# Moving tiles of the 256-column stages begin 128 bytes, not 192, past the weights' position modulo 256

## The chip, the cores and the metric

The kernel runs on one core of a Trainium2 chip. The metric is the device time of one execution in microseconds (us); the number compared is the median of several executions. The core has TensorE (PE; it loads a 128 x 128 tile of weights into its array, which the trace shows on a row of its own as PEld, and streams a moving tile past it), VectorE (DVE), ScalarE (ACT), GpSimd (POOL) and SyncE (SP), which issues most of the DMAs. Tensors in the on-chip memory have 128 partitions; an address below is the byte position in every partition.

## The reference, cut to what matters

Two transformer-like blocks over 256 tokens of width 1024. The first has one layer; the second has two layers and a second stream of 256 context tokens, which goes along through the first of them and feeds keys and values in the second. The weight products, which are nearly all of the matrix work:

```python
x = x + 0.5 * (silu(n(x) @ w_gate) * (n(x) @ w_up)) @ w_down      # 1024 -> 2816 -> 1024, six times
proj = h @ w_in[l]; ...; x = x + concat([o_a, o_b]) @ w_out[l]    # a mixer in each layer
```

The products and the result are float32.

## The kernel before, in words

**Products in three parts.** Each float32 operand is held as a high part of dtype float32r and a low part, the remainder. A weight tile of 128 x 128 meets a moving tile of 128 x n in three matmuls: high weights by high moving tile (L1464), high weights by low moving tile (L1465), low weights by high moving tile (L1466). The kind `pair` does the same on L1479 to L1481 for the first two outputs of a stage. Each matmul of the program has its own weight load, and the load of the next matmul runs beside the current one.

**Weights.** They stream from HBM in units of up to 1024 columns (`UC`) into `w_raw`, and are split by ACT (L1785) into `w_hi` and by DVE (L2085) into `w_lo`, three slots each. Most units are eight tiles of 128 columns, so tiles begin at multiples of 512 bytes. Exceptions are tiles of 96 columns (queries and keys of the second block) and of 16 (the decay projection, L1498 to L1500).

**Moving tiles.** `U` holds the normed activations, high part (`HI`) and low part (`LO`), in one of two views: `U0` and `U1`. `HH...` and `HL...` hold the hidden layer of a feed-forward part. Stages with 256 columns (one stream: the whole first block, and the second layer of the second block from its mixer on) use view `U0` and a hidden tensor allocated behind a spacer, `shift`. Stages with 512 columns (both streams) use `U1` and no spacer. For a few steps at each seam between 512-column stages the two halves of 256 columns are done one after the other, from the same unshifted tiles.

**Where tiles begin.** Tensors are allocated one behind the other, and the others before these are all whole multiples of 256 bytes long, so `U`, `w_hi` and `w_lo` begin at the same position modulo 256 (128). Within `U`, `U0` begins 48 floats, 192 bytes, later; a spacer of 48 floats does the same to the hidden tensors `f1`, `f2` and `f21`, and to the mixer tensors of the last layer (`M1`: `AC`, `FO`, `CV`, `CK`, `Y` and others). Below, **offset** means: start of the moving tile less start of the weight tile, modulo 256. It is 192 in the 256-column stages, 0 in the 512-column stages and their seams. Where the operands change places (`v_mm`, L1532 to L1534: the weights' tile moves, `U0` is loaded), the offset is 64. In `decay_mm` the 16-column weight tiles lie 64 bytes apart, so the offset goes through 192, 128, 64 and 0.

**Order of the stages.** f1 (us 16 to 198 of the profiled span), mixer 1 (to 466, with much work that is no weight product), f2 (to 651), then with 512 columns f10, mixer of layer 0, f20, f11 (to 2197), then with 256 columns mixer of layer 1 (to 2484) and f21 (to 2676). A feed-forward part is 44 outputs of 8 tiles and 8 outputs of 22 tiles, times three: 1,584 matmuls. A seam's halves have the same lines in the trace as everything else.

**What sets the order of work.** Plan writes all steps out in one list, and each engine goes through that list in order; waits are on semaphores between engines. Nothing in the list depends on addresses.

Of the kernel before, what the change touches and what calls it, by code (L numbers as in the profile page):

```python
# [9 lines left out]
F32 = mybir.dt.float32  # L10
# [1243 lines left out]
def build(nc, wstream, cols, consts, consts2, bias, xin, cvec, out):  # L1254
    with ExitStack() as stack:
        program(Plan(), nc, stack, wstream, cols, consts, consts2, bias, xin, cvec, out)


def program(plan, nc, stack, wstream, cols, consts, consts2, bias, xin, cvec, out):
    S = Signals()  # L1260
    up, at, landed = S.up, S.at, S.landed

    def sb(name, shape, dt=F32, st=None):
        return (st or stack).enter_context(nc.sbuf_tensor(name, shape, dt))

    X = sb("X", [128, 8, 512])
    U = sb("U", [128, 2 * 4096 + 64], F32R)
# [16 lines left out]

    HI = {f"U{i}": U[:, 48 - 48 * i:4144 - 48 * i].rearrange("p (k t) -> p k t", k=8) for i in range(2)}
    LO = {f"U{i}": U[:, 4144 - 48 * i:8240 - 48 * i].rearrange("p (k t) -> p k t", k=8) for i in range(2)}

    HI["UO"], LO["UO"] = HI["U0"][:, :, 256:512], LO["U0"][:, :, 256:512]  # L1290

    def shift(n, name, st):
        if n == 256:
            sb("S" + name, [128, 48], F32, st)

    def hidden(p, n):
        with ExitStack() as st:
            shift(n, p, st)
            HI[p], LO[p] = sb("HH" + p, [128, NF, n], F32R, st), sb("HL" + p, [128, NF, n], F32R, st)

    def halves(name, shape, st):
        HI[name], LO[name] = sb(name + "H", shape, F32R, st), sb(name + "L", shape, F32R, st)

# [22 lines left out]
    for l in range(2):  # L1326
# [4 lines left out]
        t2 = {}  # L1331
        with ExitStack() as st:
            shift(n, f"M{l}", st)

            t2["OT"] = []
            for half, x in (HI, "H"), (LO, "L"):
                with ExitStack() as s2:
# [5 lines left out]
            with ExitStack() as s2:  # L1343
                t2["VC"] = sb(f"VC{l}", [128, wide], F32, s2)[:, 0:3 * ns * 286].rearrange("p (c s t) -> p c s t", c=3, s=ns)
                t2["AC"] = sb(f"AC{l}", [128, 3, ns, 256], F32, s2)
            HI[f"CV{l}"] = sb(f"CVH{l}", [128, wide], F32R, st)[:, 0:3 * n].rearrange("p (c t) -> p c t", c=3)
            LO[f"CV{l}"] = sb(f"CVL{l}", [128, 3, n], F32R, st)
            def merged():
                HI[f"Y{l}"] = sb(f"Y{l}H", [128, 8, n], F32R, st)
                with ExitStack() as s4:  # L1350
                    t2["Y"] = sb(f"Y{l}", [128, 8, n], F32, s4)
                LO[f"Y{l}"] = sb(f"Y{l}L", [128, 8, n], F32R, st)

# [1274 lines left out]
```

## Time and profile before

| | us |
|---|---|
| median of 3 runs | 2685.14 |
| lowest and highest | 2680.0 and 2686.18 |
| time of the profiled execution | 2686.26 |
| its span, first to last instruction | 2684.4 |
| PE busy in it | 2594.5 (97%) |
| mean granted clock of TensorE | 0.989 |

How to read the rows further below. In the timeline a row is one matmul: start in us, duration in us, engine, line, output and inputs, count. Durations overlap, since a matmul starts while the one before is still draining; the distance from start to start is what a matmul costs when they stand one behind the other. A window's row gives its length, then for each engine busy us and number of instructions, then PE's granted clock, the DMA share and GB/s; the counts include the two or three instructions that were under way when the window began. A group's row gives line, engine, output and inputs, weight tile's and moving tile's size, count, busy us, mean ns of one, and idle time before them with what ended it. The chain is the work that ended last, followed back, in shares of the stretch by engine and line.

### The profile page before, as it was taken

How to read it: one execution, taken by the hardware profiler on the slowest of the kernel's cores; microseconds unless marked ns; L12 is line 12 of the kernel's file. 1: busy time of each engine (PE TensorE's matmuls, PEld its weight loads, DVE VectorE, ACT ScalarE, POOL GpSimd, SP SyncE). 2: the span in 40 equal slices, each digit the busy share in tenths (PEclk: the TensorE clock that was granted, in tenths of full speed). 3: DMA queues.
4: the chain of work that ended last, by engine and by line, in shares of the span. 5: the costliest groups of instructions: out<-in, count | busy, mean ns of one | idle time of the engine just before them, and what ended most of it. 6: DMA issues, size and time to landing. Idle time of an engine off the chain costs nothing.

```text
span 2684.4 us, 38719 instructions
## 1 busy us (share of the span) xinstructions
PE 2594.5 (97%) x15836; PEld 2299.7 (86%) x15836; DVE 1679.0 (63%) x2665; ACT 1094.6 (41%) x1707; POOL 64.1 (2%) x60
## 2 busy tenths in 40 slices
PE   7999898999999999999999999999999999998998
PEld 7998797999888888778888888889888888888998
DVE  6767545777677555666545767665555456776654
ACT  5446654555322224343244332224232234655543
POOL 0001030000000000000100000000000000000000
PEclk9999999999999999999999999999999999999999
DMA  7764202675555442112222455543443433244454
GB/s 262 236 231 174 88 9 72 212 237 174 167 187 190 158 143 94 51 40 87 93 89 94 149 180 185 176 159 111 146 133 130 141 110 103 74 142 161 161 181 146
DMA packets 110113, 380.98 MB, mean 142 GB/s; under 512 B 12016, under 2 KB 17392, under 8 KB 109552
## 3 DMA queue, kind: packets, MB, share of 16 engines
q1 hardware_dynamic: 108928, 373.32, 41.9%
q10 hardware_dynamic: 1008, 5.18, 0.5%
q8 instruction: 126, 2.06, 0.3%
q14 instruction: 51, 0.42, 0.1%
HBM read 377.40 MB, written 1.05 MB: 141 GB/s over the span
## 4 chain that ended last, share of the span: by engine, by line
PE 89%; DVE 5%; ACT 3%; issue 2%; DMA 0%; SPq 0%; ACTq 0%; DVEq 0%
PE B L1464 26%; PE B L1466 25%; PE B L1465 25%; ACT w_hi L1785 2%; DVE w_lo L2085 2%; PE B L1724 1%; PE B L1707 1%; PE B L1479 1%; PE B L1618 1%; PE B L1480 1%; PE B L1481 1%; PE B L1631 1%; PE B L1714 1%; DVE AC L2330 1%; DVE TMP L2112 0%
## 5 line engine op out<-in xcount | busy, mean ns | idle before, releaser
L1464 PE MATMUL B<-U,w_hi 128*128 128x256 f32 (+1 forms) x2896 | 961.7, 332 | 8.1 <-DVE w_lo L2085 8.0
L1465 PE MATMUL B<-U,w_hi 128*128 128x256 f32 (+1 forms) x2896 | 952.3, 329 | 0.0
L1466 PE MATMUL B<-U,w_lo 128*128 128x256 f32 (+1 forms) x2896 | 952.1, 329 | 0.0
L2085 DVE TENSOR_TENSOR w_lo<-w_raw,w_hi 128x1024 fp32r<-128x1024 f32 (+3 forms) x587 | 685.4, 1180 | 408.8 <-ACT w_hi L1785 407.7
L1785 ACT ACTIVATE w_hi<-w_raw 128x1024 fp32r<-128x1024 f32 (+3 forms) x587 | 590.8, 1012 | 505.3 <-PE B L1466 482.6
L1464 PEld LDWEIGHTS B<-U,w_hi 128*128 128x128 f32 x2896 | 546.1, 189 | 64.6 <-issue 8.1
L1465 PEld LDWEIGHTS B<-U,w_hi 128*128 128x128 f32 x2896 | 547.0, 189 | 53.7 <-issue 2.2
L1466 PEld LDWEIGHTS B<-U,w_lo 128*128 128x128 f32 x2896 | 545.6, 188 | 51.7
L1464 PE MATMUL B<-HHf,w_hi 128*128 128x256 f32 (+1 forms) x1122 | 364.6, 325 | 1.6 <-DVE w_lo L2085 1.6
L1466 PE MATMUL B<-HHf,w_lo 128*128 128x256 f32 (+1 forms) x1122 | 363.8, 324 | 0.0
L1465 PE MATMUL B<-HLf,w_hi 128*128 128x256 f32 (+1 forms) x1122 | 363.8, 324 | 0.0
L1848 ACT ACTIVATE HHf<-TMP 128x256 fp32r<-128x256 f32 (+1 forms) x132 | 69.3, 525 | 415.5 <-DVE TMP L2125 415.5
L1464 PEld LDWEIGHTS B<-HHf,w_hi 128*128 128x128 f32 x1122 | 211.2, 188 | 20.5 <-DVE w_lo L2085 2.2
L1465 PEld LDWEIGHTS B<-HLf,w_hi 128*128 128x128 f32 x1122 | 211.9, 189 | 18.3
L1466 PEld LDWEIGHTS B<-HHf,w_lo 128*128 128x128 f32 x1122 | 211.1, 188 | 17.8
L2125 DVE TENSOR_TENSOR TMP<-TMP,B 128x256 f32<-128x256 f32 (+1 forms) x132 | 73.1, 554 | 180.5 <-PE B L1466 177.6
L2080 DVE CUSTOM_DVE_ANT_0 w_ada<-w_ada,CS 128x1024 f32<-128x1024 f32 x144 | 175.8, 1221 | 0.0
L2078 DVE CUSTOM_DVE_ANT_0 TMP<-w_ada,CS 128x1024 f32<-128x1024 f32 x144 | 175.6, 1219 | 0.0
L2127 DVE TENSOR_TENSOR HLf<-TMP,HHf 128x256 fp32r<-128x256 f32 (+1 forms) x132 | 73.8, 559 | 78.0 <-ACT HHf L1848 78.0
L2330 DVE SCALAR_TENSOR_TENSOR AC<-VC,PC,AC 128x512 f32<-128x512 f32 (+1 forms) x180 | 103.6, 626 | 0.1
L1790 ACT ACTIVATE TMP<-X 128x256 f32<-128x256 f32 (+1 forms) x76 | 35.6, 479 | 164.4 <-DVE X L2138 145.3
L2138 DVE SCALAR_TENSOR_TENSOR X<-B,DER,X 128x256 f32<-128x256 f32 x80 | 36.2, 479 | 64.3 <-PE B L1466 64.3
(353 smaller groups left out, 2585.0 us busy)
## 6 DMA issues: line engine op xcount, KB each, us to landing
w_raw<-in_w SPq DMA_DIRECT2D x504, 512.0 KB, 4.2
w_ada<-in_w SPq DMA_DIRECT2D x144, 512.0 KB, 3.4
w_raw<-in_w SPq DMA_DIRECT2D x58, 384.0 KB, 3.2
w_raw<-in_w SPq DMA_DIRECT2D x16, 240.0 KB, 2.5
X<-in_x SPq DMA_DIRECT2D x2, 1024.0 KB, 9.7
w_raw<-in_w SPq DMA_DIRECT2D x8, 256.0 KB, 2.8
BW<-in_bias ACTq DMA_DIRECT2D x1, 1536.0 KB, 10.4
K<-in_consts ACTq DMA_DIRECT2D x2, 640.0 KB, 5.5
```

What stands on the lines that cost most here:

```text
L1464: pe.matmul(o, hi, xh, start=i == 0 and s.start, stop=False)
L1465: pe.matmul(o, hi, xl, start=False, stop=False)
L1466: e = pe.matmul(o, lo, xh, start=False, stop=i == last and s.stop)
L1785: act.activation(w_hi[:, plan.slot[u], 0:n], w_raw[:, plan.ring[u], 0:n], ACT.Copy).then_inc(*up("w_hi", u))
L1848: act.activation(HI[p][:, j, :], TM(s.t, s.n), ACT.Copy).then_inc(*up("hh", s.key))
L2078: dve.tensor_tensor_reduce(tmp[:, 5:7, :].rearrange("p a b -> p (a b)"), raw, CS[:, 0, :], 1.0, 0.0, ALU.mult, ALU.add, MOD[:, l, b, 0:1]) ...
L2080: dve.tensor_tensor_reduce(raw, raw, CS[:, 1, :], 1.0, 0.0, ALU.mult, ALU.add, MOD[:, l, b, 1:2]).then_inc(*up("ada", s.key, ("unit", u)))
L2085: dve.tensor_tensor(w_lo[:, plan.slot[u], 0:n], w_raw[:, plan.ring[u], 0:n], w_hi[:, plan.slot[u], 0:n].bitcast(F32), ALU.subtract).then_i ...
L2125: dve.tensor_tensor(h, h, PS(s.b2, s.n), ALU.mult).then_inc(*up("hm", s.key))
L2127: dve.tensor_tensor(LO[p][:, j, :], h, HI[p][:, j, :].bitcast(F32), ALU.subtract).then_inc(*up("hl", s.key))
L2138: dve.scalar_tensor_tensor(out=X[:, m, c], in0=PS(s.b)[:, c], scalar=DER[:, l, 3 + i, m, h:h + 1], in1=X[:, m, c], op0=ALU.mult, op1=ALU.a ...
L2330: dve.scalar_tensor_tensor(out=AC[:, c], in0=VC[:, c, :, i:i + 256], scalar=col(f"w_dw{l}", 31 * c + i), in1=AC[:, c], op0=ALU.mult, op1=A ...
```

## The change

The two views of `U` now lie 32 floats (128 bytes) apart instead of 48 (192 bytes), and the spacer has 32 floats. With that the offset of all 256-column stages becomes 128, that of `v_mm` 128 as well; everything at offset 0 stays. No instruction is added, removed or moved in any engine's list.

```diff
-    HI = {f"U{i}": U[:, 48 - 48 * i:4144 - 48 * i].rearrange("p (k t) -> p k t", k=8) for i in range(2)}
-    LO = {f"U{i}": U[:, 4144 - 48 * i:8240 - 48 * i].rearrange("p (k t) -> p k t", k=8) for i in range(2)}
+    HI = {f"U{i}": U[:, 32 - 32 * i:4128 - 32 * i].rearrange("p (k t) -> p k t", k=8) for i in range(2)}
+    LO = {f"U{i}": U[:, 4128 - 32 * i:8224 - 32 * i].rearrange("p (k t) -> p k t", k=8) for i in range(2)}
 
     HI["UO"], LO["UO"] = HI["U0"][:, :, 256:512], LO["U0"][:, :, 256:512]
 
     def shift(n, name, st):
         if n == 256:
-            sb("S" + name, [128, 48], F32, st)
+            sb("S" + name, [128, 32], F32, st)
```

## Rows read from the trace of the kernel before

**Rows 1.** The page: busy time by engine, then the chain by engine and line.

```profile
PE 2594.5 (97%) x15836; PEld 2299.7 (86%) x15836; DVE 1679.0 (63%) x2665; ACT 1094.6 (41%) x1707; POOL 64.1 (2%) x60
...
PE 89%; DVE 5%; ACT 3%; issue 2%; DMA 0%; SPq 0%; ACTq 0%; DVEq 0%
PE B L1464 26%; PE B L1466 25%; PE B L1465 25%; ACT w_hi L1785 2%; DVE w_lo L2085 2%; PE B L1724 1%; PE B L1707 1%; PE B L1479 1%; PE B L1618 1%; PE B L1480 1%; PE B L1481 1%; PE B L1631 1%; PE B L1714 1%; DVE AC L2330 1%; DVE TMP L2112 0%
```

**Rows 2.** Windows of 100 us in f1, in f21 and in f11.

```profile
30.00:130.00 100.00, 100.00 (x885) 100.00 (x884) 75.68 (x104) 50.36 (x75) 0.00 (x0) 1.00 0.71 232
...
2500.00:2600.00 100.00, 100.00 (x851) 100.00 (x851) 58.23 (x72) 48.35 (x72) 0.00 (x0) 1.00 0.54 185
1853.00:1953.00 100.00, 100.00 (x443) 82.79 (x442) 54.52 (x71) 30.24 (x40) 0.00 (x0) 1.00 0.43 138
```

**Rows 3.** Timeline of PE, offset 192, 256 columns: f1, then f21.

```profile
30.09 0.28 PE L1464 MATMUL B<-U,w_hi 128*128 128x256 f32 x1
...
30.77 0.28 PE L1464 MATMUL B<-U,w_hi 128*128 128x256 f32 x1
...
2519.85 0.28 PE L1464 MATMUL B<-U,w_hi 128*128 128x256 f32 x1
...
2520.91 0.28 PE L1464 MATMUL B<-U,w_hi 128*128 128x256 f32 x1
```

**Rows 4.** Timeline of PE, offset 0, 256 columns, at a seam.

```profile
655.99 0.28 PE L1481 MATMUL B<-U,w_lo 128*128 128x256 f32 x1
...
656.95 0.28 PE L1480 MATMUL B<-U,w_hi 128*128 128x256 f32 x1
```

**Rows 5.** Timeline of PE, 512 columns: offset 64, then 0, then 192.

```profile
220.42 0.39 PE L1532 MATMUL B<-w_hi,U 128*128 128x512 f32 x1
...
222.48 0.39 PE L1532 MATMUL B<-w_hi,U 128*128 128x512 f32 x1
...
1899.62 0.39 PE L1464 MATMUL B<-U,w_hi 128*128 128x512 f32 x1
...
1900.98 0.39 PE L1464 MATMUL B<-U,w_hi 128*128 128x512 f32 x1
...
2238.47 0.39 PE L1466 MATMUL B<-U,w_lo 128*128 128x512 f32 x1
...
2241.27 0.40 PE L1466 MATMUL B<-U,w_lo 128*128 128x512 f32 x1
```

**Rows 6.** Timeline of PE: decay_mm, weight tiles of 16 columns.

```profile
308.30 0.28 PE L1498 MATMUL B<-U,w_hi 128*16 128x256 f32 x1
...
310.68 0.28 PE L1498 MATMUL B<-U,w_hi 128*16 128x256 f32 x1
```

**Rows 7.** Timeline of PE at 1.2 GHz, in the first us of f1.

```profile
17.17 0.41 PE L1479 MATMUL B<-U,w_hi 128*128 128x256 f32 x1
...
17.81 0.41 PE L1479 MATMUL B<-U,w_hi 128*128 128x256 f32 x1
```

**Rows 8.** PE's groups by shape: f1, f2, mixer of layer 1, f21.

```profile
L1465 PE MATMUL B<-U,w_hi 128*128 128x256 f32 x336 | 92.7, 276 | 0.0
...
L1465 PE MATMUL B<-HLf,w_hi 128*128 128x256 f32 x176 | 48.7, 277 | 0.0
...
L1465 PE MATMUL B<-U,w_hi 128*128 128x256 f32 x280 | 78.4, 280 | 0.0
...
L1465 PE MATMUL B<-U,w_hi 128*128 128x256 f32 x336 | 94.4, 281 | 0.0
```

**Rows 9.** The chain by line: mixer of layer 1, then f21.

```profile
by line: PE B L1464 15.0%; PE B L1465 13.9%; PE B L1466 13.9%; issue 7.8%; DVE w_lo L2085 6.6%; ACT w_hi L1785 6.3%; PE B L1724 5.1%; DVE AC L2330 4.8%; PE B L1707 3.3%; PE B L1714 2.4%; DVE X L2138 1.3%; PE B L1698 1.2%; PE B L1752 1.2%; P
...
by line: PE B L1466 31.3%; PE B L1465 31.1%; PE B L1464 31.1%; DVE X L2171 1.5%; PE B L1481 0.6%; PE B L1480 0.6%; PE B L1479 0.5%; PE B L1489 0.3%; issue 0.3%; PE B L1492 0.2%; DVE SSB L2091 0.2%; ACT SSB L1807 0.2%; DVEq L2534 0.2%; ACT S
```

**Rows 10.** ACT's groups: writing U1 (around us 1030), then U0 (us 2485).

```profile
L1839 ACT ACTIVATE U<-TMP,MOD 128x256 fp32r<-128x256 f32 x16 | 7.9, 506 | 5.7 <-DVE TMP L2112 5.7
...
L1839 ACT ACTIVATE U<-TMP,MOD 128x256 fp32r<-128x256 f32 x8 | 4.0, 506 | 2.5 <-DVE TMP L2112 2.5
```

## The prediction, made before the changed kernel was run

> **What bounds the kernel now.** I read the page first: PE is busy 97% of the span and holds 89% of the chain that ended last, three quarters of it in the three lines of the weight products [rows 1]. So the time is, to first order, a number of matmuls times the distance from start to start. The change touches nothing else, and next I read that distance, stage by stage, in the timeline, and asked of each stretch what its offset is.
>
> Six matmuls of f1 at offset 192 take 30.77 - 30.09 = 0.68 us, 113.3 ns each; nine of f21, same shapes, same offset, take 1.06 us, 117.8 ns each [rows 3]. This is no accident of a moment: in 100 us f1 starts 885 matmuls and f21 only 851, PE without a gap and at full clock in both [rows 2]. At offset 0 eight take 0.96 us, 120.0 ns each [rows 4]. With 512 columns the distance is 1.36/6 = 226.7 ns at offset 0, 2.80/12 = 233 at 192 and 2.06/9 = 229 at 64 [rows 5]. At the lower clock level, 1.2 GHz, three matmuls take 0.64 us, 213.3 ns, which is 256 columns at that clock and nothing more [rows 7]. And while a weight tile of 16 columns is loaded the distance is 2.38/21 = 113.3 ns, through all four offsets, 128 among them [rows 6].
>
> So 113.3 (and twice that, 226.7) looks like the floor at 2.4 GHz, and on top of it comes something that depends on where the moving tile lies against the tile being loaded: 6.7 ns at offset 0, and at 192 either nothing or 4.5 ns. Which of the two it is does not change inside a feed-forward part (f1 and nearly all of f2 at 113.3, all of f21 at 117.8) but does from one output to the next in the mixers, where PE stops and starts. It is a rhythm that is fallen into at a start and kept; I call the two the short and the long rhythm.
>
> One rule speaks against all this. The Trainium skill (TensorE: Matmul & The Clock Gate, step 1 of Part 2) says that TensorE reads the moving tile and the next weights through two independent ports, so that loading weights takes no read bandwidth from the running matmul; by it no offset could matter and the kernel would stay at 2685. The trace disagrees: 120.0 against 113.3 ns for the same instruction at two offsets [rows 3, 4].
>
> **The change, part by part.** *What every 256-column matmul costs.* The price at offset 128 with whole weight tiles is in no row. Bounds: below, the floor, 113.3 [rows 3, 6]; above, the dearest row with these shapes, 120.0 [rows 4]. Between them I choose by a picture that the rows allow. 6.7 ns are 16 columns at 2.4 GHz, 64 bytes of a float32 tile. Let both readers walk through a ring of four places of 64 bytes each, at the same speed, and let one be held up when both stand at the same place. With 256 columns they then start nearly level: offset 0 clashes always, offset 192 (one place apart) sits at the edge of the clash and can go either way, which is the two rhythms. With 512 columns the clean offset is 0 and both neighbours, 64 and 192, cost a few ns [rows 5], so there the clash would be centred two places away, and it reaches about one place to each side. That width, put back to the 256-column case, leaves offset 128 clean with a whole place to spare on each side: one rhythm, 113.3 ns. I take the floor.
>
> *f21.* From the rise of the clock on it starts some 1,555 matmuls (336 + 176 for each of three lines, and the last of the pairs), all in the long rhythm: mean duration 281 ns where f1 has 276 [rows 8], and 4.45 ns in the distance. PE's lines are 93.5% of the chain there and more with the pairs [rows 9]: nothing covers it. 1,555 x 4.45 = 6.9 us.
>
> *f2.* Only a piece of the down product is in it: mean 277 against 276 [rows 8], 528 matmuls: 0.4 us by the rounded means, on the path.
>
> *Mixer of layer 1.* 840 matmuls on U with a mean duration of 280 [rows 8]: four of the five ns, so 80% in the long rhythm, 840 x 0.8 x 4.45 = 3.0 us; about 240 on FO, AC and CV somewhat less so, 0.6. Of this not all is on the path. The three lines are 42.8% of the 287 us in the chain [rows 9], 123 us, of some 190 us that they take (1,290 of 256 columns at 116 ns, 170 of 512 at 233): 0.65. 3.6 x 0.65 = 2.3 us. The rest is covered by the split of the weights (ACT L1785, DVE L2085) and the taps (DVE L2330), which end those waits whatever PE does.
>
> *Mixer 1.* 24 outputs of eight tiles, 576 matmuls on U. Taking half of them long, as two rhythms open at every start would have it, and 0.6 on the path: 576 x 0.5 x 4.45 x 0.6 = 0.8 us.
>
> *Moving tiles of 512 columns that shift too* (keys, values and `kr` in the last layer, `v_mm` and its like): some 190 matmuls, now at 229 to 233 [rows 5]. In the same picture 128 is the dear place for them. Bounds: all to the floor, a gain of 190 x 5 = 1.0 us; up by another 6 ns, a loss of 1.1. I take a loss of 0.2. The float32 matmuls of the last mixer whose tiles shift too (L1707, L1724) have no row that prices their offset; each is 1% of the chain [rows 1], a sixteenth of that either way would be 2 us, and I take nothing.
>
> *Seams and all 512-column stages* keep offset 0 and their distance: nothing. *ACT and DVE*, which write the shifted tiles: U1 is written in 506 ns an instruction and U0, 192 bytes on, also in 506 [rows 10]. Nothing, and they would be covered by PE in the feed-forward parts. *Waits*: none is added or removed; where PE gets faster, what is late next is the split of the weights, and f1 shows that it keeps up at 113.3 ns (no gap in 100 us [rows 2]).
>
> **Sum.** 6.9 + 0.4 + 2.3 + 0.8 - 0.2 = 10.2 us. The profiled execution took 2686.26 us (span 2684.4 and 1.9 around it), so 2676.1 us. The profile stands 1.1 us above the median of 2685.14; the short rhythm needs no luck in this case, so that is also the median I expect: 2676, 0.34% below the median before.
>
> **The rivals.**
>
> *Two rhythms stay (0.18).* If offset 128 is an edge as well, each feed-forward part again draws short or long, 6.9 us a part. For it: the before's runs lie 6.2 us apart, about one part. Against it: the edge at 192 lies next to the clash at 0, and 128 does not. Time: like before, 2685 likeliest, 2678 to 2692.
>
> *No offset matters (0.02)*, the rule above: 2685, with f21 long for another reason.
>
> *The long rhythm always (0.10).* 117.8 for every 256-column matmul. It adds 4.45 ns to 1,563 in f1, to 1,480 in f2 (13.5 us), and to the short ones of the mixers (about 880, 3.9 us, of which 0.6 count: 2.3). 2686.3 + 15.8 = 2702.
>
> *128 is as bad as 0 (0.18); this one ends slower.* If the ring has two places, not four, 128 is the same as 0. The place is the same loop; the price is 6.67 ns over the floor: f1 10.4, f2 10.0, f21 10.4 - 6.9 = 3.5, mixers 8.3 x 0.6 = 5: 28.9 us in sum, 2715. It decides as soon as the distance at offset 128 exceeds 116 ns, since the gain in f21 is then eaten by f1 and f2. For it: offsets 64 and 192 both cost with 512 columns, as they would have to. Against it: they cost unlike, 229 and 233 [rows 5], and the readers would then have no clean offset but an edge in the 256-column case, whereas f1 runs clean for 180 us.
>
> **How the numbers follow.** The clean case has 0.52, with a range of its own of 2673 to 2679: the cover in the mixers between none and whole is 5 us, the 512-column tiles 2.1. The four others have 0.18, 0.02, 0.10 and 0.18. The range goes from 2673 to 2704; only the last rival lies outside. About 0.3%, 8 us, is what a measurement of this kernel can tell from no change. The clean case is just past it, at 0.34%, and the before's own median moves with the rhythms of its runs, so I count three quarters and a bit of it as faster: 0.41, and 0.03 from lucky draws of the first rival make 0.44. Within 0.3%: 0.11 + 0.12 + 0.02 = 0.25. Slower: 0.10 + 0.18 + 0.03 = 0.31.
>
> **What the profile after would show.** Right: the three lines with a mean duration of 276 in f1, f2 and f21 alike; some 885 matmuls in every 100 us of f21; distance 120.0 still at the seams; the mixers some 3 us shorter in all. Wrong: a mean of 281 in a whole part (two rhythms, or always the long one: f1 and f2 tell which), or 283 and 120.0 ns (a ring of two); or 512-column tiles in the mixer of layer 1 far above 235 ns.

## The result, and the profile after

The changed kernel takes 2702.28 us, the kernel before in the same session 2685.66: the ratio is 1.0065, with a 95% interval of 1.0042 to 1.0089. It is slower by more than 0.3%, and the forecast was faster. 2702.28 lies inside the range given, but only by way of the rivals: the case taken as likeliest had 2673 to 2679. Run again in a later session the changed kernel took 2702.23 (e9 below).

The profiled executions took 2702.8 and 2686.26 us, 16.5 apart. First the page of the kernel after: busy time, then the chain by engine and by line.

```profile
PE 2614.2 (97%) x15836; PEld 2319.4 (86%) x15836; DVE 1678.0 (62%) x2665; ACT 1094.2 (41%) x1707; POOL 64.0 (2%) x60
...
PE 88%; DVE 6%; ACT 4%; issue 2%; DMA 0%; ACTq 0%; DVEq 0%
PE B L1464 25%; PE B L1466 25%; PE B L1465 25%; ACT w_hi L1785 2%; DVE w_lo L2085 2%; PE B L1724 1%; PE B L1707 1%; PE B L1479 1%; PE B L1618 1%; PE B L1480 1%; PE B L1481 1%; PE B L1631 1%; PE B L1714 1%; DVE AC L2330 1%; DVE TMP L2112 0%
```

The counts are those of [rows 1], and PE is busy 19.7 us longer: no work was added, some of it costs more. Next the windows of 100 us, in f1, f2 and f21.

```profile
30.00:130.00 100.00, 100.00 (x845) 100.00 (x844) 72.14 (x99) 47.46 (x71) 0.00 (x0) 1.00 0.64 218
480.00:580.00 100.00, 100.00 (x845) 100.00 (x844) 71.80 (x98) 48.49 (x72) 0.00 (x0) 1.00 0.64 216
2530.00:2630.00 100.00, 100.00 (x845) 100.00 (x844) 57.74 (x70) 47.08 (x71) 0.00 (x0) 1.00 0.54 184
```

All three now have 845 matmuls, at full clock and without a gap, where f1 had 885 and f21 851 [rows 2]. The timeline of PE in f1 gives the distance.

```profile
59.79 0.28 PE L1464 MATMUL B<-U,w_hi 128*128 128x256 f32 x1
59.91 0.28 PE L1465 MATMUL B<-U,w_hi 128*128 128x256 f32 x1
60.02 0.28 PE L1466 MATMUL B<-U,w_lo 128*128 128x256 f32 x1
60.15 0.28 PE L1464 MATMUL B<-U,w_hi 128*128 128x256 f32 x1
60.27 0.28 PE L1465 MATMUL B<-U,w_hi 128*128 128x256 f32 x1
60.38 0.28 PE L1466 MATMUL B<-U,w_lo 128*128 128x256 f32 x1
...
61.57 0.28 PE L1464 MATMUL B<-U,w_hi 128*128 128x256 f32 x1
```

Fifteen matmuls in 1.78 us are 118.67 ns each. The distances in it are uneven and come back every five: 115, 118, 122, 120 and 119 ns by the records. This is neither of the two rhythms before, 113.3 and 117.8 [rows 3], but a third, and all three feed-forward parts are in it, from a few matmuls behind the start to the end.

The two mixers, before (first fence) and after (second), each from the first matmul behind one feed-forward part to the first of the next; the number behind the counts is the granted clock.

```profile
198.72:466.19 267.47, 235.91 (x1792) 218.45 (x1793) 155.19 (x304) 150.66 (x295) 43.48 (x34) 0.95 0.25 87
2197.08:2485.92 288.84, 265.01 (x1888) 240.61 (x1886) 198.32 (x380) 157.42 (x260) 7.40 (x10) 0.97 0.39 124
```

```profile
207.72:474.72 267.00, 236.66 (x1791) 218.80 (x1792) 153.74 (x304) 150.56 (x295) 43.41 (x34) 0.96 0.25 87
2212.84:2500.87 288.03, 265.60 (x1888) 241.27 (x1886) 198.24 (x380) 157.07 (x260) 7.38 (x10) 0.99 0.38 125
```

So the 16.5 us are +9.0 in f1 (178.6 to 187.6), -0.5 in mixer 1, +7.3 in f2 (184.3 to 191.6), -0.1 over everything from there to us 2197, -0.8 in the mixer of layer 1 and +1.6 in f21 (190.2 to 191.8). The distance explains the three parts: 1,563 x 5.33 ns = 8.3 us in f1 (0.7 more: at its start the matmuls stay at 213 ns until us 21.8, before until 20.0; e9 doesn't have this: +8.2), 1,556 x 5.13 = 8.0 in f2 (0.7 less: the stops inside it came out shorter, one in its down product at 0.77 us from start to start instead of 1.12), 1,558 x 0.89 = 1.4 in f21. What has to be found out is why offset 128 costs 118.67 ns, and why two mixers with dearer matmuls are not longer.

### The profile page after: what moved, and what is told of

It is laid out like the page before. It is cut to its first block, busy times and chain, and to the rows that moved or that the text cites. A ratio compares the mean times of both kernels' runs of the same rounds, so it can differ in the third digit from the quotient of the medians.

```text
span 2701.0 us, 38719 instructions
## 1 busy us (share of the span) xinstructions
PE 2614.2 (97%) x15836; PEld 2319.4 (86%) x15836; DVE 1678.0 (62%) x2665; ACT 1094.2 (41%) x1707; POOL 64.0 (2%) x60
## 4 chain that ended last, share of the span: by engine, by line
PE 88%; DVE 6%; ACT 4%; issue 2%; DMA 0%; ACTq 0%; DVEq 0%
PE B L1464 25%; PE B L1466 25%; PE B L1465 25%; ACT w_hi L1785 2%; DVE w_lo L2085 2%; PE B L1724 1%; PE B L1707 1%; PE B L1479 1%; PE B L1618 1%; PE B L1480 1%; PE B L1481 1%; PE B L1631 1%; PE B L1714 1%; DVE AC L2330 1%; DVE TMP L2112 0%
## 5 line engine op out<-in xcount | busy, mean ns | idle before, releaser
L2125 DVE TENSOR_TENSOR TMP<-TMP,B 128x256 f32<-128x256 f32 (+1 forms) x132 | 73.2, 554 | 184.3 <-PE B L1466 181.7
## 6 DMA issues: line engine op xcount, KB each, us to landing
BW<-in_bias ACTq DMA_DIRECT2D x1, 1536.0 KB, 10.4
```

The source lines that it names most:

```text
L2125: dve.tensor_tensor(h, h, PS(s.b2, s.n), ALU.mult).then_inc(*up("hm", s.key))
```

## The experiments

**e1_map: the price of an offset, by itself.** A small program that leaves out the whole computation: it copies its input to the output and runs matmuls in the kernel's pattern. Each of 16 moving tensors holds its tiles at one offset:

```python
wh, wl = (t[:, shift // 4 + 128 * k:shift // 4 + 128 * k + m] for t in W[0])
h, l = (M[o][:, o // 4 + 512 * j:o // 4 + 512 * j + n] for j in (k % 2, 2 + k % 2))
yield wh, h, k == 0, False
yield wh, l, False, False
yield wl, h, False, k == 7
```

> This kernel leaves the whole computation out: it copies the input to the output and runs products in three parts (24 matmuls an output, as L1464 to L1466 do) at chosen offsets, so only the distance from start to start is read. Theory 1 (the price is a function of the offset, moving tile less weight tile, modulo 256, and of the number of columns): with 256 columns 120.0 ns at 0, 118.7 at 128, 113.3 or 117.8 at 192, as in the two kernels; with the weights 64, 128 or 192 bytes up, the same prices at the same differences. Theory 2 (the moving tile's own position counts): with the weights moved the prices stay where the moving tile is. For offset 64, which no 256-column stage had: theory 1a, that 64 and 192 are mirror images, gives 113.3 or 117.8; theory 1b, that the price falls steadily from 0 over 64 and 128 to 192, gives 119.3. With 512 columns 226.7 at 0, 233 at 192. After a stop, at 192, both 113.3 and 117.8 should occur over eight outputs; at 128 and 0 one level each.

Measured, 72 matmuls of 256 columns on each offset without a stop. The timeline of PE in this program, the first matmul of a group and that of the next one (m64B is the tensor with offset 64):

```profile
60.05 0.28 PE L66 MATMUL B<-m0B,wh 128*128 128x256 f32 x1
...
68.69 0.28 PE L66 MATMUL B<-m16B,wh 128*128 128x256 f32 x1
...
94.16 0.28 PE L66 MATMUL B<-m64B,wh 128*128 128x256 f32 x1
...
102.32 0.28 PE L66 MATMUL B<-m80B,wh 128*128 128x256 f32 x1
...
127.75 0.28 PE L66 MATMUL B<-m128B,wh 128*128 128x256 f32 x1
...
136.28 0.28 PE L66 MATMUL B<-m144B,wh 128*128 128x256 f32 x1
...
161.86 0.28 PE L66 MATMUL B<-m192B,wh 128*128 128x256 f32 x1
...
170.34 0.28 PE L66 MATMUL B<-m208B,wh 128*128 128x256 f32 x1
```

8.64 us / 72 = 120.0 ns at offset 0, 8.16 / 72 = 113.3 at 64, 8.53 / 72 = 118.5 at 128, 8.48 / 72 = 117.8 at 192. All sixteen, the first matmuls of each left out (ns):

| offset | 0 | 16 | 32 | 48 | 64 | 80 | 96 | 112 | 128 | 144 | 160 | 176 | 192 | 208 | 224 | 240 |
|---|---|---|---|---|---|---|---|---|---|---|---|---|---|---|---|---|
| 256 columns | 120.0 | 118.7 | 116.7 | 118.3 | 113.3 | 120.0 | 120.0 | 113.3 | 118.6 | 118.6 | 117.3 | 119.3 | 117.8 | 119.2 | 118.3 | 117.2 |
| 512 columns | 226.7 | | 233.3 | | 228.9 | | 233.3 | | 233.3 | | 234.3 | | 233.3 | | 233.3 | |

The map has no wide valley and no wide hill, as the four places of 64 bytes would give it. It has single cheap places between dear ones, and 128 is not one of them. Three more things come out of the same program. With the weights 64, 128 or 192 bytes higher the price goes with the difference of the two addresses, not with either (difference 0: 120.0 ns each time; 128: 118.7 each time; 64: 117.8 each time; 192: 113.3, 117.8 and 113.3). With 128 columns the distance is 111.67 ns at all four offsets tried. And with weight tiles of 16 or 32 columns it is 113.33 ns at each of 0, 64, 128 and 192, with 64 columns 113.3, 116.7, 116.7 and 119.3. The timeline for 16 columns at offset 128, first matmul and the first of the next offset:

```profile
639.47 0.28 PE L91 MATMUL B<-m128B,wh 128*16 128x256 f32 x1
...
644.94 0.28 PE L91 MATMUL B<-m192B,wh 128*16 128x256 f32 x1
```

5.47 us for 48, 114 ns, of which the first few still run in the rhythm before; then 113.33. So the price needs both a moving tile and a wide weight load beside it, which fits two readers meeting; how they meet isn't shown. And the 21 matmuls of `decay_mm` [rows 6], which the prediction took as a sign that offset 128 can be had at the floor, could not have shown anything else. With a stop before every output, eight times each, offset 0 had 120.0 and 128 had 118.7 ns every time, as expected; 192 had 113.3 eight times of eight, where both rhythms had been expected.

**e2_off64: the whole kernel at offset 64**, cheap in the map.

```diff
-    HI = {f"U{i}": U[:, 48 - 48 * i:4144 - 48 * i].rearrange("p (k t) -> p k t", k=8) for i in range(2)}
+    HI = {f"U{i}": U[:, 16 - 16 * i:4112 - 16 * i].rearrange("p (k t) -> p k t", k=8) for i in range(2)}
...
-            sb("S" + name, [128, 48], F32, st)
+            sb("S" + name, [128, 16], F32, st)
```

> The whole kernel with U0 and the spacer at 16 floats: offset 64 in the 256-column stages. Theory 1a (mirror of 192): 113.3 or 117.8 ns a matmul, 2676 to 2697 us, likeliest near 2686. Theory 1b (steady fall from 0 to 192): 119.3 ns, 6 ns more on some 3,100 matmuls of f1 and f2 and 1.5 on f21, 2706 to 2709 us.

Measured: 2696.79 us, ratio 1.004 (1.002 to 1.006), at the upper end of the 2676 to 2697 expected and not near 2686. The windows in f1, f2 and f21 have 851 matmuls each, 117.8 ns; of 56 starts in the whole kernel 50 are at 117.8 and 6 at 113.3. In the map's part with a stop before every output offset 64 had 117.8 eight times of eight, and only the group that ran on from another offset had 113.3. The profile of the kernel before, counted in the same way, has 27 starts at 113.3 and 28 at 117.8. So there are two rhythms at 64 too, and a start almost always gives the dear one, while at 192 it gave either about as often: what a map shows without stops is not what a kernel gets.

**e3_off0: the whole kernel at offset 0**, the dearest place: the views of `U` coincide, the spacer is 256 bytes.

```diff
-    HI = {f"U{i}": U[:, 48 - 48 * i:4144 - 48 * i].rearrange("p (k t) -> p k t", k=8) for i in range(2)}
+    HI = {f"U{i}": U[:, 0:4096].rearrange("p (k t) -> p k t", k=8) for i in range(2)}
...
-            sb("S" + name, [128, 48], F32, st)
+            sb("S" + name, [128, 64], F32, st)
```

> The whole kernel with no shift: offset 0 in every stage. If the seams' 120.0 ns is the price of offset 0 in general and not of the seams, f1, f2 and f21 run at 120.0 ns and the time is 2715 us by the sum made for the rival of the prediction. If the seams have their price from something else (halves of a wider tile, other buffers), the stages keep 113.3 or 117.8 and the time is 2676 to 2697.

Measured, in one execution: 2703.64 us. Windows of this kernel in f1, in f21 and in the two mixers:

```profile
30.00:130.00 100.00, 100.00 (x836) 100.00 (x835) 71.24 (x98) 47.23 (x70) 0.00 (x0) 1.00 0.67 217
...
2530.00:2630.00 100.00, 100.00 (x836) 100.00 (x835) 57.28 (x70) 46.11 (x69) 0.00 (x0) 1.00 0.56 183
...
209.10:473.70 264.60, 235.96 (x1791) 218.30 (x1792) 153.95 (x304) 150.50 (x295) 44.01 (x34) 0.96 0.26 88
2211.91:2499.85 287.94, 266.28 (x1887) 242.31 (x1886) 198.19 (x380) 156.96 (x260) 7.36 (x10) 0.99 0.40 125
```

836 in 100 us are the 120.0 ns of the seams [rows 4]. The three feed-forward parts cost 10.4 + 9.0 + 3.5 = 22.9 us more than before, close to the 23.9 of the prediction's sum for this rival. But the mixers, for which it had 5 us more, are 2.9 and 0.9 us shorter.

**e4_weights64up: the price goes with the difference.** Everything is as before the change, but `U`, `w_hi` and `w_lo` move against each other: a gap of 16 floats stands ahead of `w_hi` and `w_lo`, so that 192 becomes 128 in the 256-column stages, and 0 becomes 192 in the 512-column ones.

```diff
-    PC = sb("PC", [128, 64 * math.ceil(ncol / 64)])
...
+    sb("GAP", [128, 16])
...
+    PC = sb("PC", [128, 64 * math.ceil(ncol / 64) - 16])
```

> The kernel before with w_hi and w_lo 64 bytes up and all moving tiles where they were: offset 128 in the 256-column stages, 192 in the 512-column stages, 192 at the seams. Theory 1 (the offset counts): f1, f2, f21 at 118.7 ns as in the changed kernel, 512 columns at some 233 ns instead of 226.7, so 5,300 x 6.3 = 33 us more on top of 2702: 2730 to 2740 us. Theory 2 (the moving tile's own position counts): no matmul changes, 2680 to 2690 us.

Measured, in one execution: 2743.93 us, 4 above the range expected. With 512 columns 430 matmuls start in 100 us, 233 ns instead of 226.7, and the stretch from the seam behind f2 to the last mixer is 34.7 us longer (1581.3 for 1546.6). f2 and f21 run at 118.67 ns, as in the kernel after, although no view has moved: it is the difference that counts, in the kernel as in the small program. f1 runs at 120.0, 2 us more than was expected: offset 128 has a second, dearer rhythm.

**e5_starts: all offsets in steps of 8 bytes, six starts each**, every output of 24 matmuls behind a stop of another length. It also leaves the computation out.

```python
for i in range(total):
    n = 40 + 61 * (i % 7)      # ACT keeps PE waiting with a copy of n columns
    act.wait_ge(s_p, i + 1)
    act.activation(SC[:, 0:n], X[:, 0:n], ACT.Copy).then_inc(s_s, 1)
```

> Like the first map this kernel leaves the computation out and only copies the input; 256 columns, 128-column weights, one output of 24 matmuls after each stop, six stops of different lengths for each case. Theory: a start falls into one of a few rhythms, and which are open depends on the offset: at 0 only 120.0 ns, at 128 118.7 (rarely 120.0), at 64 117.8 and rarely 113.3, at 192 both 117.8 and 113.3. Rival: the offset alone sets the price and the length of the stop nothing, so all six starts of a case agree. Offset 112 (113.3 ns in its one stretch of the first map): if it has one rhythm, six of six at 113.3; if it was luck, some of 116 to 120. Where high and low moving tile have different offsets, or the low weights another position: the price of a mixed case should lie between those of its two offsets if each matmul pays for itself (0 with 192: 115 to 119), and may be 113.3 in some if the rhythm is what counts.

Measured, distance behind each start, the first eight matmuls left out (ns): offset 0: 120.0 six times; 64: 117.8 six times; 112: 113.3 to 114.5 six times, the only one of the 32 that is near the floor whenever it starts; 128: 118.7 six times; 192: 113.3 four times, 117.7 twice. The offsets that are no multiple of 16 lie at 117 to 123, most of them at 120. With the high and the low tile at different offsets it is 116.5 to 122, with the low weights alone moved 113.3 to 122.3. Two starts at offset 192 in the timeline, a few rows of each:

```profile
587.39 0.50 PE L76 MATMUL B<-m192B,wh 128*128 128x256 f32 x2 [0.58 <-ACT SC L61]
587.74 0.28 PE L76 MATMUL B<-m192B,wl 128*128 128x256 f32 x1
...
590.12 0.28 PE L76 MATMUL B<-m192B,wl 128*128 128x256 f32 x1
591.03 0.50 PE L76 MATMUL B<-m192B,wh 128*128 128x256 f32 x2 [0.63 <-ACT SC L61]
591.37 0.28 PE L76 MATMUL B<-m192B,wl 128*128 128x256 f32 x1
...
593.84 0.28 PE L76 MATMUL B<-m192B,wl 128*128 128x256 f32 x1
```

From the first `wl` to the last are 21 matmuls: 2.38 us (113.3 ns) in one start, 2.47 us (117.6) in the next. The addresses and the instructions are the same; PE had stood still for 0.58 us and 0.63 us. So the rhythm is drawn at the start, and which ones come up depends on the offset.

**e6_off112: the whole kernel at offset 112**, the place that e5 names. The hidden tensors are cut out of wider ones instead of standing behind a spacer; the last mixer's own tensors stay at 192.

```diff
+    HI = {f"U{i}": U[:, 28 - 28 * i:4124 - 28 * i].rearrange("p (k t) -> p k t", k=8) for i in range(2)}
...
+            at0 = 28 if n == 256 else 0
+            for half, x in (HI, "HH"), (LO, "HL"):
+                tile = sb(x + p, [128, NF * n + (64 if at0 else 0)], F32R, st)
+                half[p] = tile[:, at0:at0 + NF * n].rearrange("p (k t) -> p k t", k=NF)
```

> The whole kernel with U0 and the hidden tensors of 256 columns at offset 112 (28 floats; slices of slightly larger tensors), the other tensors of the last mixer left at 192. If 112 has only the rhythm of 113.3 ns: f1, f2 and f21 all with a mean duration of 276 ns, and 2686 - 7 (f21) - 1 to 3 in the mixers = 2675 to 2679 us in every run. If it has several, as 192 has: 2677 to 2700 us and different parts at different levels.

Measured: 2679.34 us against 2680.48 of the kernel before in that session, ratio 0.9992 (0.9977 to 1.0007); 2675 to 2679 in every run was expected, and five of the ten lie above that, up to 2682.87. Its windows in f1, f2, f21 and the mixer of layer 1:

```profile
30.00:130.00 100.00, 100.00 (x885) 100.00 (x884) 75.47 (x105) 50.14 (x75) 0.00 (x0) 1.00 0.71 233
...
480.00:580.00 100.00, 100.00 (x885) 100.00 (x884) 77.47 (x108) 50.03 (x74) 0.00 (x0) 1.00 0.73 234
2530.00:2630.00 100.00, 100.00 (x884) 100.00 (x884) 58.75 (x72) 48.95 (x69) 0.00 (x0) 1.00 0.60 194
...
2197.81:2485.51 287.70, 263.72 (x1888) 239.38 (x1886) 198.00 (x380) 157.35 (x260) 9.37 (x10) 0.98 0.39 125
```

All three parts are at the floor, f21 8 us shorter than in the profile before. Its ten executions lie within 5.4 us, the thirteen of the kernel before in that session within 19.4 (2674.33 to 2693.71). The median hardly moves, although f21 alone is worth 8 us against the profile before. The median of the kernel before was 2685.66, 2686.54, 2680.48 and 2680.24 in the four sessions; that it draws its rhythms anew in each execution, and beside e6 mostly the short one, is argued from these times, since only one of its executions was traced. e1 to e4, e5 and e6, and e7 to e9 ran on three different chips, which is a rival for the 6 us between its medians; against it stands the changed kernel with 2702.28 and 2702.23 us in two sessions, whose rhythm was the same in both traces. This is the steadier kernel; that it is the faster one is not shown.

**e7_views_only, e8_spacer_only, e9_after_again: the change in its two halves, and whole.**

```diff
# e7: the views of U alone
+    HI = {f"U{i}": U[:, 32 - 32 * i:4128 - 32 * i].rearrange("p (k t) -> p k t", k=8) for i in range(2)}
...
# e8: the spacer alone
+            sb("S" + name, [128, 32], F32, st)
```

> Only the two views of U are moved to offset 128; the spacer keeps 48 floats, so the hidden tensors and the last mixer's own tensors stay at offset 192. Theory 1 (each matmul pays by the offset of its own moving tile, the mixers hide it): gate and up products of f1, f2 and f21 (1,056 matmuls a part) at 118.67 ns, so f1 +5.6 us, f2 +5.3, f21 +0.9, together 11.8 of the 16.5 us that the whole change cost; the down products (528 a part) at 192 fall into 113.3 or 117.8, which adds 0 to 4.7 us over f1 and f2. Mixers within 1 us of before. Ratio near 1.005. Theory 2 (the loss is a state of the whole program, or comes from the mixers): no stage has a distance of its own for each half of its products, and the ratio is 1.000 or that of the whole change, 1.0065.

> Only the spacer is changed: hidden tensors and the last mixer's own tensors at offset 128, U stays at 192. Theory 1: down products of f1, f2 and f21 at 118.67 ns, +2.8, +2.4 and +0.5 us, 5.7 in sum, and the gate and up products at 113.3 or 117.8 whatever the start gives them. Ratio near 1.002, and this run and the one with the views alone add up to the whole change when the rhythms at 192 are the same. Theory 2: as above, 1.000 or 1.0065.

> The changed kernel once more, in the same job as its two halves. Theory 1: 118.67 ns in f1, f2 and f21 again, mixers within 1 us of before, ratio 1.0065 (1.004 to 1.009). Theory 2 (offset 128 has several rhythms too, as 192 has, and the run shown had the dear one by chance): at least one part at another distance, and a median that differs by 5 us or more.

Measured, against 2680.24 us: e7 2701.41, ratio 1.0078 (1.0062 to 1.0095); e8 2690.57, 1.0035 (1.0023 to 1.0047); e9 2702.23, 1.0081 (1.0066 to 1.0096). Windows of the kernel with the views alone: f1 in its gate and up products, then in its down products.

```profile
30.00:130.00 100.00, 100.00 (x836) 100.00 (x835) 71.94 (x99) 47.48 (x71) 0.00 (x0) 1.00 0.67 220
153.00:193.00 40.00, 40.00 (x355) 40.00 (x354) 25.34 (x34) 17.95 (x22) 0.00 (x0) 1.00 0.67 225
```

And the same two of the kernel with the spacer alone:

```profile
30.00:130.00 100.00, 100.00 (x852) 100.00 (x851) 73.07 (x100) 48.57 (x72) 0.00 (x0) 1.00 0.69 226
153.00:193.00 40.00, 40.00 (x336) 40.00 (x335) 24.43 (x32) 16.78 (x21) 0.00 (x0) 1.00 0.64 210
```

Each half of the products pays by its own offset, inside one part and without a stop between: in e7 the products on `U` (offset 128) are at 120.0 ns in f1 and 118.67 in f2 and f21, the hidden ones (192) at 113.4, 114.6 and 113.35; in e8 the hidden ones (128) are at 120.0 in f1, then 118.7 and 118.7, and those on `U` (192) at 117.6, 113.35 and 117.8. That settles where the loss sits. The sizes missed: 120.0 was not expected in f1, and both ratios are higher than the expected 1.005 and 1.002. By its ratio alone, 1.0078, e7 could not be told from the whole change, and the two halves do not add up to it (0.78% and 0.35% against 0.81%), since in each of them the products left at 192 can draw the long rhythm; it is the windows that decide. The profile of e7 is its fastest execution, 2693.83 us; the three others took 2701.1 to 2702.0. If their hidden products drew the long rhythm, 527 x (4.4 + 3.2 + 4.4) ns = 6.3 us of these 7.3 to 8.1 would be theirs; only the one trace was taken, so this is argued. e9 repeats the first result in every part: 118.66 ns in f1, f2 and f21. So no seldom draw made the kernel after slow; with both halves at 128, eight executions in two sessions lie between 2700.5 and 2703.7.

**The mixers through all runs.** Length of the mixer of layer 1, mean distance of its 256-column matmuls at full clock, and the time in which PE is busy there at the lower clock level, from the traces:

| | mean distance, ns | PE busy at 1.2 GHz, us | length, us |
|---|---|---|---|
| e6, offset 112 | 115.0 | 11.6 | 287.7 |
| before, 192 | 116.1 | 11.3 | 288.8 |
| e8, spacer alone | 117.1 | 12.9 | 289.5 |
| e2, 64 | 117.3 | 12.9 | 289.7 |
| e7, views alone | 118.0 | 8.0 | 287.9 |
| after, 128 | 118.9 | 5.1 | 288.0 |
| e9, 128 again | 118.8 | 5.0 | 287.9 |
| e3, 0 | 119.8 | 4.9 | 287.9 |

Up to 117.3 ns the length rises with the distance. Above, it falls back, and with it goes the time at the lower level, from 11.3 to 12.9 us down to 4.9 to 8.0. A matmul at 1.2 GHz takes 213.3 ns [rows 7], so 6.2 us less there, from before to after, are about 3 us won. Against that, an estimate: 1,290 matmuls 2.8 ns dearer, times the share of 0.65 that the prediction had, are 2.3 us lost. In mixer 1 the time at the lower level is 20.5 us before, 15.8 after, 13.7 at offset 0.

## Why the prediction was wrong, step by step

**What bounds the kernel: right.** The time is the number of matmuls times a distance that depends on the offset. Every stage that didn't change its offset kept its time (1546.63 and 1546.55 us from the seam behind f2 to us 2197), and the parts that did moved by count times distance.

**The price at offset 128: this step failed.** The prediction had bounds of 113.3 and 120.0 and chose 113.3, "by a picture that the rows allow": a ring of four places of 64 bytes, whose width was read from the 512-column case and put back to the 256-column case. The measured price is 118.67, in one feed-forward part of some runs 120.0. e1 and e5 show that the price isn't a smooth function of the distance on a ring: it changes from 113.3 to 120 in 8 or 16 bytes, places of 64 bytes don't show, and 256 columns and 512 columns have different cheap places. Three known offsets could not give the fourth. The one row that seemed to speak for the floor at 128 [rows 6] had weight tiles of 16 columns, and e1 shows that these cost nothing at any of the four offsets.

**The sum.** f21: forecast -6.9, measured +1.6. f2: -0.4, measured +7.3. f1 was at the floor and was left out of the sum, since nothing could be won there: +9.0. The asymmetry was in view: two of three parts stood at the floor, where a move could only lose, and in the third only 6.9 us could be won. A choice between two bounds should have weighed that.

**The mixers, -2.3 and -0.8: mis-sized.** Their own terms counted only cheaper matmuls times a share of 0.65 and 0.6 on the path. Measured is -0.8 and -0.5, with dearer matmuls. Two things were left out: the cover is not a fixed share, and the granted clock did not stay as it was (0.97 before and 0.99 after in the mixer of layer 1). The chain by line of the mixer of layer 1, after:

```profile
by line: PE B L1464 13.7%; PE B L1466 13.0%; PE B L1465 12.9%; issue 8.3%; ACT w_hi L1785 7.3%; DVE w_lo L2085 6.8%; PE B L1724 5.0%; DVE AC L2330 4.8%; PE B L1707 3.3%; PE B L1714 1.8%; DVE X L2138 1.4%; ACT L2056 1.3%; DVE TMP L2112 1.3%;
```

The three lines have 39.6% of it, 114 us, where they had 42.8% [rows 9], although each matmul takes longer; ACT's split of the weights and issue took their place. A clock that stays up longer where PE's matmuls follow one another with less idle time between them fits the four dear rows of the table against the four cheap ones; among the cheap ones it is not ordered by the distance (11.3 to 12.9 us), and it was not tried by itself, so it stays argued.

**The 512-column tiles that shift, a loss of 0.2: measured about nothing.** The tiles of `v_mm` went from 229.1 to 232.2 ns (47 of them), those of the mixer of layer 1 from 233.0 to 231.7 (118): in sum nothing. The picture behind the term, 128 as the dear place, isn't borne out: e1 has 233.3 ns at 128 as at 32, 96, 192 and 224. The float32 matmuls L1707 and L1724, put at nothing, kept their distance of 429 and 112 ns.

**The rivals.** "The long rhythm always" gave 2702 and the time is 2702.3, but by two errors that cancel: its distance was 117.8 (measured 118.67, which adds 0.89 ns x 3,043 = 2.7 us in f1 and f2, and 1.4 in f21), its mixers +2.3 (measured -1.3). "128 is as bad as 0" had the distance nearly right, 120.0, and 2715; e3, which is that case in earnest, took 2703.6: 8.8 of the 11.4 us by which the sum was too high are the mixers, which it had at +5 and which measured -3.8. Its point of decision, 116 ns, was passed, though by the prediction's own counts the gain in f21 is eaten up at 115 already (3,043 x 1.7 ns lost against 1,555 x 2.8 won). "Two rhythms stay" is right in that offset 128 has two, 118.67 and 120.0, and wrong in that neither is cheap.

**No offset matters.** The trace and e1 to e8 speak against it: 113.3, 117.8, 118.7 and 120.0 ns for the same instruction. The Trainium skill (TensorE: Matmul & The Clock Gate, Part 2, step-by-step) gives TensorE two independent read ports, one for the moving tile and one for the weights; with weight tiles of 16 or 32 columns these runs agree, with tiles of 128 columns they do not, and the measurement decides. The same page (Part 1, "Wait — 56ns, not 53.3ns?") puts the distance at the high clock at N / 2.4 plus some 2.5 ns, which makes an estimate of 109.2 for 256 columns; no run here had a distance below 113.3 with 256 columns. At the lower level the page has N / 1.2, and both agree on 213.3.

**The signs that the prediction named.** PE's groups by shape of the kernel after, two of f1 and one of the mixer of layer 1, to be laid beside [rows 8]:

```profile
L1465 PE MATMUL B<-U,w_hi 128*128 128x256 f32 x336 | 94.5, 281 | 0.0
L1465 PE MATMUL B<-HLf,w_hi 128*128 128x256 f32 x176 | 49.5, 281 | 0.0
...
L1465 PE MATMUL B<-U,w_hi 128*128 128x256 f32 x280 | 79.2, 283 | 0.0
```

281 in f1, where it was 276, shows the miss at once. But by the sign as it was put, "281 in a whole part", this would be the long rhythm, and it isn't: the mean duration is 281 ns at 117.8 and at 118.67 ns alike. Only the count in 100 us (851 or 845) and the timeline tell the two apart.

## What to carry to other kernels

Where a moving tile of float32r lies against the weight tile that is loaded beside it can be worth 6% of every matmul (113.3 against 120.0 ns), so measure it offset by offset before a layout is chosen, in steps of 16 bytes, with the kernel's own widths, pattern and stops: a price from another tile size or from a run without stops does not carry over. A part that already stands at the floor can only lose by a move; price it first. And take a stage's matmul savings for the stage's time only where PE holds the chain without waits: in the mixers 3 ns more a matmul made neither of them longer.

## What was not expected of the hardware

- The distance has a few fixed levels, which come back to 0.02 ns in parts of 1,500 matmuls and in every run: 113.33, 117.78, 118.67 and 120.0 ns for 256 columns; 118.67 is a cycle of five uneven distances. By arithmetic the two in the middle are mixes of the outer ones: one part of 113.33 and two of 120.0 make 117.78, one and four make 118.67. The single distances in the records don't show such steps, so it stays arithmetic. The level is drawn where PE starts after a stop and mostly kept, even through 180 us.
- Offset 112 gives 113.3 to 114.5 ns in six starts of six, its neighbours at 104 and 120 bytes give 120 and more.
- Weight tiles of 16 and 32 columns cost nothing at the four offsets tried; from 64 columns on the offset has a price.
- With 512 columns only offset 0, of eight tried, gives 226.7 ns; 64 gives 228.9 and the others 233 to 234.
- Offset 0, 22.9 us dearer in its feed-forward parts, costs only some 17 us in the whole kernel (one execution, 2703.64 against the 2686.26 of the profile before): the mixers give back 3.8, and the stretch with 512 columns 1.6, which in this execution has no time at the lower clock level where the profile before has 3.4 us.

What makes the levels, and why 112 is cheap, no run here tells.
